# The last two down units and the final norm over three parts of the tokens (256, 128, 128)

## The reference, cut to what matters

```
act = gelu(up[..., :D_FF_2], approximate=True) * up[..., D_FF_2:]
x = x + act @ w_down[l]          # 2816 -> 1024 features
...
return rms_norm_2(x, g_final)    # x * rsqrt(mean(x*x over features) + 1e-6) * g_final
```

## Time and profile before

| | |
|---|---|
| median of 3 runs | 1869.73 us (1869.22 to 1870.35) |
| the profiled execution: its own time | 1870.59 us |
| the profiled execution: span of its trace | 1868.4 us |
| granted clock of PE, mean | 0.997 |
| PE busy | 1851.8 us, 99% of the span |
| PEld busy | 1482.3 us, 79% |
| DVE busy | 1207.1 us, 65% |
| ACT busy | 559.4 us, 30% |
| POOL busy | 15.8 us, 1% |
| DMA over the span | 194.65 MB, 104 GB/s on average |
| `last_pair` begins on PE, last product begins | 1842.36 and 1858.57 us |
| last `scaled` of DVE begins | 1865.3 us |

### The profile page before, as it was taken

The page is one execution under the profiler, slowest core; times in us unless marked ns, Lnnn a source line. Parts: engine busy times, 40 slices in busy tenths (PEclk is TensorE's granted clock), DMA queues, the critical chain, the costliest instruction groups (busy, mean ns, idle before and its releaser), DMA issues.

```text
span 1868.4 us, 21625 instructions
## 1 busy us (share of the span) xinstructions
PE 1851.8 (99%) x8656; PEld 1482.3 (79%) x8656; DVE 1207.1 (65%) x1589; ACT 559.4 (30%) x533; POOL 15.8 (1%) x58
## 2 busy tenths in 40 slices
PE   8999999999999999999999999999999999999998
PEld 6888888878888778888888888877778888888877
DVE  6764667657745476443244779979975777635765
ACT  5333222222232332221122111148851133222321
POOL 0000000000000000000000000000000000000000
PEclk9999999999999999999999999999999999999999
DMA  5224341463111332222322224232224222223222
GB/s 205 90 81 155 110 161 65 147 244 123 69 68 46 115 133 90 90 88 84 121 90 73 85 90 158 91 107 83 84 71 152 102 90 90 85 95 108 86 71 73
DMA packets 49158, 194.65 MB, mean 104 GB/s; under 512 B 6721, under 2 KB 17345, under 8 KB 34369
## 3 DMA queue, kind: packets, MB, share of 16 engines
q1 hardware_dynamic: 49088, 193.70, 29.9%
HBM read 180.84 MB, written 12.85 MB: 104 GB/s over the span
## 4 chain that ended last, share of the span: by engine, by line
PE 97%; DVE 2%; issue 1%; DMA 0%; ACT 0%; SPq 0%; POOLq 0%; POOL 0%; DVEq 0%
PE bank L982 30%; PE bank L984 30%; PE bank L983 30%; PE xb L1310 2%; DVE wlo L1383 1%; PE xb L1021 0%; PE xb L1256 0%; PE xb L1246 0%; PE bank L1153 0%; PE bank L1154 0%; PE bank L1155 0%; PE xb L1264 0%; PE xb L1014 0%; DMA raw<-in_up 0%; PE xb L1214 0%
## 5 line engine op out<-in xcount | busy, mean ns | idle before, releaser
L982 PE MATMUL bank<-uhi,whi 128*128 128x512 f32 x1552 | 622.6, 401 | 7.1 <-DVE wlo L2269 6.9
L664 ACT ACTIVATE whi<-raw 128x2048 fp32r<-128x2048 f32 (+3 forms) x177 | 299.8, 1694 | 1088.4 <-PE bank L984 1050.2
L984 PE MATMUL bank<-uhi,wlo 128*128 128x512 f32 x1552 | 616.6, 397 | 0.0
L983 PE MATMUL bank<-ulo,whi 128*128 128x512 f32 x1552 | 616.4, 397 | 0.0
L1383 DVE TENSOR_TENSOR wlo<-raw,whi 128x2048 fp32r<-128x2048 f32 (+3 forms) x177 | 356.6, 2014 | 83.2 <-ACT whi L664 81.1
L982 PEld LDWEIGHTS bank<-uhi,whi 128*128 128x128 f32 x1552 | 293.2, 189 | 80.1 <-issue 9.6
L984 PEld LDWEIGHTS bank<-uhi,wlo 128*128 128x128 f32 x1552 | 293.1, 189 | 71.5
L983 PEld LDWEIGHTS bank<-ulo,whi 128*128 128x128 f32 x1552 | 293.5, 189 | 71.0 <-issue 1.4
L982 PE MATMUL bank<-hhi,whi 128*128 128x512 f32 (+1 forms) x548 | 213.4, 389 | 0.8 <-DVE wlo L1383 0.4
L983 PE MATMUL bank<-hlo,whi 128*128 128x512 f32 (+1 forms) x548 | 212.6, 388 | 0.0
L984 PE MATMUL bank<-hhi,wlo 128*128 128x512 f32 (+1 forms) x548 | 212.6, 388 | 0.0
(11 more groups left out here) (396 smaller groups left out, 1806.4 us busy)
## 6 DMA issues: line engine op xcount, KB each, us to landing
raw<-in_up SPq DMA_DIRECT2D x65, 1024.0 KB, 4.8
raw<-in_win SPq DMA_DIRECT2D x16, 1024.0 KB, 4.8
raw<-in_wout SPq DMA_DIRECT2D x8, 1024.0 KB, 4.8
raw<-in_down1a SPq DMA_DIRECT2D x8, 768.0 KB, 4.3
tab<-tab_kept SPq DMA_DIRECT2D x4, 1536.0 KB, 8.7
raw<-in_down2a SPq DMA_DIRECT2D x8, 768.0 KB, 4.3
raw<-in_down3a SPq DMA_DIRECT2D x8, 768.0 KB, 4.3
raw<-in_down1b SPq DMA_DIRECT2D x8, 640.0 KB, 3.9
```

Source lines behind the costliest of these rows:

```text
L664: act.activation(whi[s][:, 0:width], raw[s][:, 0:width], ACT.Copy).then_inc(w_hi, 1)
L982: pe.matmul(dst, wh, hi, start=first, stop=False)
L983: pe.matmul(dst, wh, lo, start=False, stop=False)
L984: return pe.matmul(dst, wl, hi, start=False, stop=last)
```

## The change

`PARTS` gives the last pair three parts of 256, 128 and 128 tokens in place of two of 256. Everything in `last_pair` goes by these parts: products, sums, spreads, `add_in`, means, root, `scaled`, and the stores of SP. Part 2 shares the banks of part 0 (other columns). The slots on PE, the order on DVE, POOL's calls and the count of stores are written anew.

```diff
+PARTS = (slice(0, 2 * P), slice(2 * P, 3 * P), slice(3 * P, S))
...
+        def part_of(s, t):
+
+            at = PARTS[t].start if t == 2 else 0
+            return DB[s][t % 2][:, at:at + PARTS[t].stop - PARTS[t].start]
...
-            for t in range(2):
-                tok = slice(t * S // 2, (t + 1) * S // 2)
+            for t, tok in enumerate(PARTS):
                 for k in range(0, KD, 2):
                     sp.wait_ge(out_ready, KD * t + k + 2)
                     sp.dma_start(out[k * P:(k + 2) * P, tok].rearrange("(m p) s -> p m s", p=P), x[:, k:k + 2, tok])\
                         .then_inc(stored, 16)
-            sp.wait_ge(stored, 16 * KD)
+            sp.wait_ge(stored, 16 * len(PARTS) * KD // 2)
...
-            inverse_root(2, 2)
+            inverse_root(1, 2)
+            inverse_root(1, 3)
...
-                for t in range(2):
-                    tok = slice(t * S // 2, (t + 1) * S // 2)
+                slots = {(0, 1, 6): lambda: part_sums(0, acc, acc_ready, nacc),
+                         (1, 0, 8): lambda: part_sums(0, sq, last_sq, n_sq),
+                         (1, 1, 8): lambda: part_sums(1, acc, acc_ready, nacc),
+                         (2, 0, 1): lambda: part_spread(0),
+                         (2, 0, 6): lambda: part_sums(1, sq, last_sq, n_sq),
+                         (2, 1, 4): lambda: part_spread(1),
+                         (2, 1, 8): lambda: part_sums(2, acc, acc_ready, nacc)}
+                for t, tok in enumerate(PARTS):
...
-                            last = product(DB[s][t][:, 0:S // 2], (whi[s], wlo[s]), slice(k * P, (k + 1) * P),
+                            last = product(part_of(s, t), (whi[s], wlo[s]), slice(k * P, (k + 1) * P),
                                            hhi[:, k, tok], hlo[:, k, tok], k == 0, k == tiles - 1)
                         last.then_inc(tail_out, 1)
-                half_sums(1, sq, last_sq, n_sq)
-                half_spread(1)
+                part_sums(2, sq, last_sq, n_sq)
+                part_spread(2)
...
                 add_in(0, 1)
-                half_root(0)
+                part_root(0)
                 add_in(1, 0)
-                dve.wait_ge(spread, n_spread.step())
-                scaled(0, range(6))
                 part_means(1)
                 add_in(1, 1)
+                dve.wait_ge(spread, n_spread.step())
+                scaled(0, range(0, 2))
+                part_root(1)
+                scaled(0, range(2, 4))
+                add_in(2, 0)
+                scaled(0, range(4, 5))
+                part_means(2)
+                scaled(0, range(5, 6))
+                add_in(2, 1)
                 scaled(0, range(6, KD))
-                half_root(1)
+                part_root(2)
                 dve.wait_ge(spread, n_spread.step())
                 scaled(1, range(KD))
+                dve.wait_ge(spread, n_spread.step())
+                scaled(2, range(KD))
```

More of the change, by code:

```diff
@@ L1066, in last_pair, with part_sums, part_spread @@
                         for k in range(tiles):
[L1067 to L1072, removed]
-                            last = product(DB[s][t][:, 0:S // 2], (whi[s], wlo[s]), slice(k * P, (k + 1) * P),
+                            if (t, j, k) in slots:
+                                slots[t, j, k]()
+                            last = product(part_of(s, t), (whi[s], wlo[s]), slice(k * P, (k + 1) * P),
                                            hhi[:, k, tok], hlo[:, k, tok], k == 0, k == tiles - 1)
                         last.then_inc(tail_out, 1)
-                half_sums(1, sq, last_sq, n_sq)
-                half_spread(1)
+                part_sums(2, sq, last_sq, n_sq)
+                part_spread(2)
             n_sq = Tally(last_sq)
-            def half_sums(t, src, ready, tally):
+            def part_sums(t, src, ready, tally):
                 pe.wait_ge(ready, tally.step())
-                for c in range(2 * t, 2 * t + 2):
+                for c in range(PARTS[t].start // P, PARTS[t].stop // P):
                     at = c if src is acc else 4 + c
-                    last = pe.matmul(XB[2 * t][:, at:at + 1], src[:, c * P:(c + 1) * P], ones[:, 0:1],
+                    last = pe.matmul(XB[2 * (t % 2)][:, at:at + 1], src[:, c * P:(c + 1) * P], ones[:, 0:1],
                                      start=True, stop=True)
                 last.then_inc(sums_out, 1)
-            def half_spread(t):
+            def part_spread(t):
                 pe.wait_ge(rs_ready, n_root.step())
-                for c in range(2 * t, 2 * t + 2):
-                    last = pe.matmul(XB[2 * t + 1][:, c * P:(c + 1) * P],
+                for c in range(PARTS[t].start // P, PARTS[t].stop // P):
+                    last = pe.matmul(XB[2 * (t % 2) + 1][:, c * P:(c + 1) * P],
                                      nstat[:, c:c + 1].broadcast_to([P, P]), ident[:, :], start=True, stop=True)
@@ L1608, in add_in @@
                 def add_in(t, j):
-                    m, tok = KD - 2 + j, slice(t * S // 2, (t + 1) * S // 2)
+                    m, tok = KD - 2 + j, PARTS[t]
                     dve.wait_ge(tail_out, 2 * t + j + 1)
-                    then(tt(out=x[:, m, tok], in0=DB[(nb + j) % 2][t][:, 0:S // 2], in1=x[:, m, tok], op=ALU.add))
+                    then(tt(out=x[:, m, tok], in0=part_of((nb + j) % 2, t), in1=x[:, m, tok], op=ALU.add))
                     square = tt(out=sq[:, tok], in0=x[:, m, tok], in1=x[:, m, tok], op=ALU.mult)
@@ L1619, in part_means, with part_root @@
                 def part_means(t):
+                    c0, c1 = PARTS[t].start // P, PARTS[t].stop // P
                     dve.wait_ge(sums_out, n_norm.step())
-                    ts(nstat[:, 4 + 2 * t:6 + 2 * t], XB[2 * t][:, 2 * t:2 * t + 2], 1.0 / D, EPS, ALU.mult, ALU.add)
-                def half_root(t):
+                    ts(nstat[:, 4 + c0:4 + c1], XB[2 * (t % 2)][:, c0:c1], 1.0 / D, EPS, ALU.mult, ALU.add)
+                def part_root(t):
+                    c0, c1 = PARTS[t].start // P, PARTS[t].stop // P
                     dve.wait_ge(sums_out, n_norm.step())
-                    stt(out=nstat[:, 2 * t:2 * t + 2], in0=XB[2 * t][:, 4 + 2 * t:6 + 2 * t], scalar=1.0 / D,
-                        in1=nstat[:, 4 + 2 * t:6 + 2 * t], op0=ALU.mult, op1=ALU.add).then_inc(rt_ready, 1)
+                    stt(out=nstat[:, c0:c1], in0=XB[2 * (t % 2)][:, 4 + c0:4 + c1], scalar=1.0 / D,
+                        in1=nstat[:, 4 + c0:4 + c1], op0=ALU.mult, op1=ALU.add).then_inc(rt_ready, 1)
                 def scaled(t, ms):
-                    tok = slice(t * S // 2, (t + 1) * S // 2)
+                    tok = PARTS[t]
                     for m in ms:
-                        stt(out=x[:, m, tok], in0=x[:, m, tok], scalar=col("g_final_2", m), in1=XB[2 * t + 1][:, tok],
-                            op0=ALU.mult, op1=ALU.mult).then_inc(out_ready, 1)
+                        stt(out=x[:, m, tok], in0=x[:, m, tok], scalar=col("g_final_2", m),
+                            in1=XB[2 * (t % 2) + 1][:, tok], op0=ALU.mult, op1=ALU.mult).then_inc(out_ready, 1)
                 add_in(0, 0)
```

## The result

The changed kernel takes 1875.95 us (median of 8 runs, 1874.92 to 1876.24), the one before 1870.04 in the same comparison (8 runs, 1869.07 to 1871.61). The ratio is 1.0031, with an interval of 1.0022 to 1.0040: slower by 4 to 7.5 us. The span of the profiled execution is 1873.7 us in place of 1868.4, its own time 1875.8.

The account below looks back on a forecast made before the run. PE's stream was taken as the bound, then a serial 9.83 us chain behind its last product. +6.84 for PE, -1.2 for the chain and -0.3 for stores gave +5.3: median 1875.0 us, range 1871.0 to 1877.5.

Parts of the forecast that it names:

- step of a 128-column product: PE, parts 1 and 2: products come 0.112 us apart, set by weight loads; bounds 0.059 (columns only) and 0.188 (loads not overlapped).
- products from the second half's or part 1's first to the last: PE's stretch after 1850.27: 119 steps of 0.112 plus 16 inserted passes, 1.81, makes 15.14 us in place of 8.30.
- waits of PE in front of sums and spreads there: PE before the last product: each sum or spread has over 1.3 us in hand, so no wait is added.
- last product begins, root: End of PE's stream and DVE's root behind it: last product 6.84 us later, at 1865.41; root at 1867.06.
- last spread under `scaled` of part 1: Chain's end: last spread done by 1869.1, hidden under part 1's eight `scaled` ending 1869.3, by 0.1 in the worst case.
- sixteen `scaled`, DVE's end: DVE after the last root: sixteen 128-wide `scaled`, 0.26 us apart, some 4.2 us, ending at 1871.4 where it was 1865.78.
- store of 128 KB: Last stores: 2.0 us each, 0.3 back, no queue at one every 0.52 us; both ends kept, -0.6 to +2.
- span: Profiled execution: +6.84 for PE, -1.2 for the chain, -0.3 for stores, +5.3 in all, 1873.7 us.
- median: Whole kernel's time: 1869.7 + 5.3 = 1875.0 us; by the profiled execution's own time 1875.9.
- Rival 1: PE, 128-column products: columns alone set the step (0.059), loads hide; result -0.8, 1868.9 us; chance 0.13.
- Rival 2: PE, parts 1 and 2: granted clock falls to the lower level, 12 us more, 1887; chance 0.05.
- Rival 3: End: stores of 512-byte rows queue or a PE slot is missed, 1876 to 1877.5 us; counted inside the forecast's 0.80.

Follow-up runs that it names:

- experiments 1 to 3: Changed kernel, products of parts 1 and 2 with 64 moving columns, 64 weight columns, or 256 moving columns; one execution each, spans 1883.2, 1866.4, 1874.5 us.
- experiment 5: Against the kernel before: last pair's products in three parts (256, 128, 128), everything behind them in two halves of 256; ratio 1.0036, length 31.97 us.
- experiment 1: Changed kernel with 64 moving columns in place of 128 in the products of parts 1 and 2; one execution, span 1883.2 us.
- experiment 2: Changed kernel with 64 weight columns in place of 128 in the products of parts 1 and 2; one execution, span 1866.4 us, length 25.22.
- Experiment 7: Against the kernel before: products in halves, second half's sums, roots, spreads in two parts of 128, six of eight `scaled` 256 wide; ratio 0.9997, length 25.29 us.

## Why the prediction was right

| step | predicted | measured |
|---|---|---|
| step of a 128-column product | 0.112 | 0.112 |
| products from the second half's or part 1's first to the last | 15.14 | 15.02 (1850.39 to 1865.41) |
| waits of PE in front of sums and spreads there | none | none, PE and PEld busy 15.20 of 15.20 |
| last product begins, root | 1865.41, 1867.06 | 1865.41, 1867.05 |
| last spread under `scaled` of part 1 | at the latest 0.1 before it is wanted | done at 1868.38, wanted after eight `scaled`, about 1869.2 |
| sixteen `scaled`, DVE's end | 4.2, 1871.4 | 4.21, 1871.33 |
| store of 128 KB | 2.0, no queue | 2.0 (1.9 at the least), none |
| span | 1873.7 | 1873.7 |
| median | 1875.0 | 1875.95 |

The step on which all hung was the choice of 0.112 between 0.059 and 0.188. It was taken from loads of 128 weight columns beside other work (one column moving; float32 scores), and experiments 1 to 3 show that it was right for that reason: at full clock the step doesn't care for 64 or 128 moving columns, and it falls to 0.060 with half of the weights. Here the trace agrees with the load rule of the Trainium skill, "TensorE: Matmul & The Clock Gate", section "LDWEIGHTS (loading the stationary operand)": by P/1.2 the estimate is 107 ns for 128 weight columns, beside 0.112 measured, and 53 ns for 64, which then lies under the 0.060 of the columns. The sustained 81 ns at N=128 of the same page of the Trainium skill (section "Back-to-back issue gap") does not hold for these float32r products, which came 0.112 apart.

What was inexact: the stretch was 0.12 shorter than predicted and began 0.12 later, so the exact 1865.41 is partly chance. The median rose by 5.9 where I had 5.3. The lengths of the two traces differ by 5.17. The chain of before that I started from held 0.35 of low clock at its last spread, which the changed kernel hides; with that spread at full clock, as in experiment 5, the difference would be 5.5. The rest lies ahead of the last pair or in the scatter of the runs (the interval allows 4 to 7.5). The baseline moved as well: its median was 1869.73 in the runs shown and 1870.04 in the comparison. That rest I did not settle.

Rival 1 (free loads) is refuted for 128 weight columns, and its price bears out: length 25.22 where loads were halved, 0.8 under before, of which 0.35 is again before's low clock. Rival 2 (the clock) did not happen in the changed kernel, but experiment 1 shows that it is no idle worry: with half of the columns again the length was 41.06, about 10 us more. Rival 3 found nothing to queue: 128 KB stores landed in 2.0.

## What to carry to other kernels

- A split that makes products narrower has a price as soon as the moving operand no longer covers its weight load. Read the load's own distance from a place where nearly nothing moves (sums by a column of ones), divide by the time of a column, and keep products above that width; here 0.112 / 0.46 ns, an estimate of about 240 columns.
- Before splitting an end finer, work out what the end could gain if the split were free. Here that was 0.8 us (experiment 2), against the 6.7 by which the last product came later.
- Split what is serial and cheap (sums, root, spread) and leave whole what is paid by the instruction: DVE's 128-wide `scaled` took 0.26 where half of a 256-wide one is 0.2. Experiment 7 does so and is 0.75 under before in its trace, which is less than the runs can tell.

## What the runs showed of the hardware that I had not expected

- The granted clock fell to 0.50 while PE was never idle: with 128x128 weights loaded every 0.112 us and 64 columns moving, in the one execution of experiment 1. With 128 columns at the same distance it stayed at 1.00 over 15.2 us. A PE that reads as fully busy is not safe from the lower level.
- At the lower level the distance of the loads went from 0.112 to 0.213, and one load's record from 0.19 to 0.33, with only 64 columns moving: the load slows with the granted clock as the products do.
- The small products behind the last big one ran at full clock in some executions and near the lower level in others, 0.71 or 1.06 for the same four passes. An end that waits for them has that scatter of 0.35 us; the changed kernel, which covers its last spread with `scaled`, does not wait for it.
